# Attention's units laid between the slabs of the scan's r, k and v, in an encoder block on one core

## The reference, cut to what matters

```python
h_in = rms_norm(x, norm1_w)
z = h_in @ w_in                        # 4608 attention, 3360 scan, 4096 gate columns
z_attn, z_rwkv, z_gate = split(z)
# attention: 3 groups (dilation 1, 4, 16) of 8 heads of 64; q, k RMS-normed per head
for g, (window, dilation) in enumerate(((128, 1), (512, 4), (2048, 16))):
    o_g, lse_g = dilated_band_attention(q[:, :, g], k[:, :, g], v[:, :, g], dilation, 64, slopes[g])
o_attn = sum_g softmax_over_groups(lse)[g] * o_g
# scan: r, k, v and LoRA inputs are shifted over tokens; kk = k * k_k, unit length per head
zr = token_shift_centred(z_rwkv); ...
wkv = rwkv7_bidir_scan(r, decay, k_dir, v, kk, iclr)      # 16 heads, two directions
...
gates = sigmoid(z_gate + b_gate)       # 32 slabs of 128 columns
x = x + (gates[0] * (o_attn @ w_a) + gates[1] * (o_rwkv @ w_b)) @ w_out
x = x + swiglu(rms_norm(x, norm2_w))
```

## Time and profile before

| | |
|---|---|
| Device time, median of 3 runs | 3886.76 us (3876.7 to 3889.54) |
| The profiled execution | 3877.64 us |
| Its span, first to last instruction | 3875.9 us |
| Mean granted TensorE clock | 0.933 |
| PE busy | 3538.8 us, 91% |
| PE weight loads, DVE, ACT, POOL busy | 2882.6, 1642.1, 1056.4, 1637.7 us |
| DMA | 405.91 MB, mean 105 GB/s |

### The profile page before, as it was taken

The page is one execution under the profiler, slowest core; times in us unless marked ns, Lnnn a source line. Parts: engine busy times, 40 slices in busy tenths (PEclk is TensorE's granted clock), DMA queues, the critical chain, the costliest instruction groups (busy, mean ns, idle before and its releaser), DMA issues. The chain is left out here.

```text
span 3875.9 us, 45226 instructions
## 1 busy us (share of the span) xinstructions
PE 3538.8 (91%) x16478; PEld 2882.6 (74%) x16478; DVE 1642.1 (42%) x2026; ACT 1056.4 (27%) x1621; POOL 1637.7 (42%) x1347
## 2 busy tenths in 40 slices
PE   5999999886668899999857799999999999999999
PEld 4477788675545788888735577888888888888887
DVE  3066715663246777777523244332133123302321
ACT  4332211212332344444322212222222112212221
POOL 2133344231002877787713444344444444444433
PEclk8799999996558999999978999999999999999999
DMA  4433344331005555555243334233333333333333
GB/s 160 151 105 93 94 133 121 106 111 57 24 24 137 126 136 130 130 148 130 60 141 95 114 103 123 84 97 89 106 97 94 89 109 90 91 99 98 97 91 104
DMA packets 765541, 405.91 MB, mean 105 GB/s; under 512 B 191390, under 2 KB 726106, under 8 KB 764922
## 3 DMA queue, kind: packets, MB, share of 16 engines
q1 hardware_dynamic: 765434, 404.53, 36.1%
HBM read 345.73 MB, written 58.72 MB: 104 GB/s over the span
## 5 line engine op out<-in xcount | busy, mean ns | idle before, releaser
L131 POOL TENSOR_TENSOR w_lo_b<-w_raw_b,w_hi_b 128x2048 fp32r<-128x2048 f32 (+3 forms) x200 | 744.0, 3720 | 1014.0 <-ACT w_hi_b L124 1013.8
L140 PE MATMUL f_bank<-act_rounded,w_lo_b 128*128 128x512 f32 x1664 | 649.6, 390 | 21.6 <-POOL act_rounded L1896 13.8
L141 PE MATMUL f_bank<-act_rounded,w_hi_b 128*128 128x512 f32 x1664 | 648.8, 390 | 0.0
L142 PE MATMUL f_bank<-act_rounded,w_hi_b 128*128 128x512 f32 x1664 | 648.7, 390 | 0.0
L124 ACT CAST w_hi_b<-w_raw_b 128x2048 fp32r<-128x2048 f32 (+3 forms) x200 | 312.9, 1565 | 929.3 <-PE f_bank L142 858.6
L131 POOL TENSOR_TENSOR w_lo<-w_raw,w_hi 128x2048 fp32r<-128x2048 f32 x63 | 290.3, 4609 | 572.8 <-ACT w_hi L124 572.8
L140 PE MATMUL bank<-h_hi,w_lo 128*128 128x512 f32 x1008 | 404.8, 402 | 20.4 <-POOL w_lo L131 13.8
L142 PE MATMUL bank<-h_hi,w_hi 128*128 128x512 f32 x1008 | 395.7, 393 | 0.0
L141 PE MATMUL bank<-h_lo,w_hi 128*128 128x512 f32 x1008 | 395.5, 392 | 0.0
L140 PEld LDWEIGHTS f_bank<-act_rounded,w_lo_b 128*128 128x128 f32 x1664 | 313.3, 188 | 88.4 <-POOL act_rounded L1896 14.2
L142 PEld LDWEIGHTS f_bank<-act_rounded,w_hi_b 128*128 128x128 f32 x1664 | 313.2, 188 | 65.2
(11 more groups left out here) (319 smaller groups left out, 5444.2 us busy)
## 6 DMA issues: line engine op xcount, KB each, us to landing
w_raw<-in_w_in_dram SPq DMA_DIRECT2D x63, 1024.0 KB, 5.3
w_raw_b<-in_w_ffn_gate_dram SPq DMA_DIRECT2D x44, 1024.0 KB, 5.1
w_raw_b<-in_w_ffn_up_dram SPq DMA_DIRECT2D x44, 1024.0 KB, 5.2
w_raw_b<-in_w_ffn_down_dram SPq DMA_DIRECT2D x64, 704.0 KB, 4.5
gate_w_plain<-in_w_in_dram SPq DMA_DIRECT2D x64, 512.0 KB, 4.5
w_raw_b<-in_w_out_dram SPq DMA_DIRECT2D x16, 1024.0 KB, 5.7
zt<-out SPq DMA_DIRECT2D x60, 256.0 KB, 2.6
zt<-lout SPq DMA_DIRECT2D x40, 256.0 KB, 2.0
```

Of the source, the lines that this page charges most:

```text
L131: pool.tensor_tensor(g.w_lo[n.slot][:, 0:k, :], g.w_raw[n.slot][:, 0:k, :], g.w_hi[n.slot][:, 0:k, :].bitcast(F32), ALU.subtract).then_inc ...
L140: pe.matmul(bank, wl, hi[:, ka, :], start=start and j == 0, stop=False)
L141: pe.matmul(bank, wh, lo[:, ka, :], start=False, stop=False)
L142: ins = pe.matmul(bank, wh, hi[:, ka, :], start=False, stop=stop and j == len(ks) - 1)
```

## The change

The r, k and v slabs leave `phase_project` and go, with five slabs of the gates, into a new `phase_attention` of 29 slots with one slab each. Slots 0 to 11 also take scores, soft and exp of two units each, and the transpose, the weighted values and `file` of the two units before; slots 13, 15 and 16 (with 14 on DVE) the merge. Scores (`sc_ps`), `s_sb` and `p_t` have one buffer instead of two. Slabs come as p-th of r, p-th of k, p-th of v; a k slab's norm (`heads`, `floor`, `root`, `unit`) is done two slots later. Weights come in halves through a ring of five raw and four high halves. The order on each engine is written out per slot. Distances, slopes and masks are built at the end of `phase_setup` on POOL, after its two low parts. The scan keeps 27 gate slabs, so its last ten slots have none (before: five).

```diff
 def phase_setup(...):       # POOL
                 for c in range(2):
                     split_lo(pool, g, Step(c), KD)
+                attention_consts(pool, g, att_consts, dist_abs)
+                scan_masks(pool, g, made_masks)
...                          # DVE, after its last subtraction
+                dve.wait_ge(att_consts, 7)
+                for v in (g.dist[:, 0:3, :], g.dist[:, 3:5, 0:P]):
+                    dve.scalar_tensor_tensor(out=v, in0=v, scalar=-1.0, in1=v, op0=ALU.mult, op1=ALU.max).then_inc(dist_abs, 1)
...
-    NA, NB = 36, 24
-                (SB0, 8, "shift", COL_RKV, ROW_RKV, 24, None, 0),
-                (SB0 + 8, 8, "shift norm", COL_RKV + RW, ROW_RKV + RW, 24, "k_k", 8),
-                (SB0 + 16, 8, "shift", COL_RKV + 2 * RW, ROW_RKV + 2 * RW, 32, None, 16))
...
+N_SLAB = 3 * NPAIR
+EARLY_GATES = 5
+NGATE = 32 - EARLY_GATES
...
+N_SLOT = N_SLAB + EARLY_GATES
+RING = 5
+MERGE = N_ATT // 2 + 1
+
+def att_pe(s):
+    first = [("open", s, 4 if s == 0 else 0)]
+    if is_key(s - 2):
+        first.append(("heads", s - 2, 0))
+    for n in units_in(s):
+        first.append(("scores", n, 2))
+    for n in units_in(s - 1):
+        if n % ATT_PER_PAIR == 0:
+            j = n // ATT_PER_PAIR
+            first += [("turn_v0", j, 1), ("turn_v12", j, 1)]
+        first += [("turn_p", n, 4), ("sum", n, 0)]
+    if s == MERGE:
+        first += [("turn_rows", gr, 2) for gr in range(3)]
+    if s == MERGE + 2:
+        first += [("spread", n, 2) for n in range(8)]
+    if s == MERGE + 3:
+        first += [("spread", n, 2) for n in range(8, N_BC)]
+    return first
+
+def att_dve(s):
+    if 0 <= s - 1 < N_SLOT:
+        stages.append(("shift" if s - 1 < N_SLAB else "gate", s - 1))
+    if is_key(s - 2):
+        stages.append(("floor", s - 2))
+    for n in units_in(s):
+        stages.append(("soft", n))
+    for n in units_in(s - 1):
+        stages.append(("file", n))
+    if is_key(s - 2):
+        stages.append(("unit", s - 2))
...
+def att_act(s):
+    if is_key(s - 2):
+        stages.append(("root", s - 2))
+    for n in units_in(s):
+        if n % ATT_PER_PAIR == 0:
+            stages.append(("by_residue", n // ATT_PER_PAIR))
+    for i, n in enumerate(units_in(s - 1)):
+        if n % ATT_PER_PAIR == 0:
+            j = n // ATT_PER_PAIR
+            stages += [("take_v0", j), ("take_v12", j)]
+        stages.append(("take_p", n))
+        if i == 0:
+            stages.append(("high", 2 * s + 3))
+    if not units_in(s - 1):
+        stages.append(("high", 2 * s + 3))
+    for n in units_in(s):
+        stages.append(("exp", n))
+    if is_key(s - 1):
+        stages.append(("square", s - 1))
...
+    stages.append(("high", 2 * s + 4))
...                          # SP, per slot
+                    weights(2 * s + 4)
...                          # loads of the next pair's q, k, v
+                    weights(2 * s + 5)
+                    if 0 <= s - 1 < N_SLOT:
+                        sp.wait_ge(taken_dve, freed(x))
+                        sp.dma_start(zt[row:row + P, :], out[x % 2][:, :]).then_inc(out_stored[x % 2], 16)
+                    if is_key(s - 2):
+                        sp.wait_ge(taken_dve, ATT_DVE_AT["unit", s - 2])
...                          # DVE, soft
+                            dve.wait_ge(made, ATT_PE_AT["scores", n])
+                            if n >= 1:
+                                dve.wait_ge(taken_act, ATT_ACT_AT["exp", n - 1])
...                          # PE: scores, then sum
+                            if n >= 1:
+                                pe.wait_ge(taken_dve, ATT_DVE_AT["soft", n - 1])
...
+                            pe.wait_ge(taken_act, ATT_ACT_AT["take_p", n])
+                            if n >= 1:
+                                pe.wait_ge(taken_dve, ATT_DVE_AT["file", n - 1])
```

More of the change, by code:

```diff
@@ L590, in norm, with turn @@
                     link(dve.tensor_tensor(y[:, :], y[:, :], t_sb[:, :], ALU.mult))
[L591 to L604, removed]
+                    if not first:
+                        slot_free(st)
+                    dve.scalar_tensor_tensor(out=out[st.slot][:, :], in0=raw[st.slot][:, :], scalar=param(g, w),
+                                             in1=y[:, :], op0=ALU.mult, op1=ALU.mult).then_inc(g.out_ready, 1)
+                def turn(base, i, norms, w, first=False):
                     for j in range(UN):
@@ new lines, in att_dve @@
+def att_dve(s):
+    stages = []
+    if 0 <= s - 1 < N_SLOT:
[8 more added lines that the diff above has]
+        stages.append(("unit", s - 2))
+    if s == MERGE:
+        stages += [("rows", gr) for gr in range(3)] + [("less_top", gr) for gr in range(3)]
+    if s == MERGE + 1:
+        stages.append(("share", 0))
+    if s == MERGE + 2:
+        stages += [("weigh", n) for n in range(8)]
+    if s == MERGE + 3:
+        stages += [("weigh", n) for n in range(8, N_BC)]
+    return stages
@@ new lines, in att_act @@
+def att_act(s):
+    stages = []
+    if is_key(s - 2):
[16 more added lines that the diff above has]
+        stages.append(("square", s - 1))
+    if s == MERGE:
+        stages += [("exp_top", gr) for gr in range(3)]
+    stages.append(("high", 2 * s + 4))
+    return stages
@@ L1230, in phase_attention, with att_counts @@
+def att_counts(stages):
+    counts = {}
+    for s in range(N_SLOT + 1):
+        for st in stages(s):
+            if st[0] not in ("high", "open"):
+                counts[st[0], st[1]] = len(counts) + 1
+    return counts
+ATT_PE_AT, ATT_DVE_AT, ATT_ACT_AT = (att_counts(f) for f in (att_pe, att_dve, att_act))
+def phase_attention(nc, g, a, zt, oat):
+    w_in = a["w_in"].rearrange("l (k p) n -> (l p) k n", p=P)
     NP = ATTN_HPG // 2
+    H = ATTN_HPG
+    NH = 2 * N_SLOT
     with ExitStack() as ctx:
@@ new lines, in phase_attention, with two_banks @@
+        spare = [v for t in (s_sb, *p_sb, p_t) for v in halves(t)]
+        m_row, d_row, m_top, total = spare[0:3], spare[3:6], spare[6], spare[7]
+        def two_banks(t):
+            v = t[:, :, :].rearrange("p a b -> p (a b)")
+            return v[:, 0:SEQ], v[:, SEQ:2 * SEQ]
+        row_banks = (two_banks(sc_ps), two_banks(pt_ps), (pv_ps[:, :], heads_ps[:, :]))
+        spread_banks = two_banks(sc_ps) + two_banks(pt_ps)
+        made, taken_dve, taken_act, chain = sem("att_made"), sem("att_taken_dve"), sem("att_taken_act"), sem("att_chain")
@@ L1303, in _ @@
[L1303 to L1313 removed]
+                for h in range(NH):
+                    pool.wait_ge(hi_ready, h + 1)
+                    pool.tensor_tensor(raw_half(w_lo, h), raw_half(w_raw, h), hi_half(h).bitcast(F32), ALU.subtract).then_inc(lo_ready, 1)
```

781 lines of the change are left out of this document (425 added, 356 removed).

## The result

The changed kernel takes **3869.93 us** (median, 3855.48 to 3875.67, 14 runs), the kernel before 3894.69 us on the same chip (3874.58 to 3900.37, 14 runs): a ratio of **0.9938, 95% interval 0.9921 to 0.9955**. It gains 25 us where 78 were forecast, outside the range of 3750 to 3852. The profiled execution has a span of 3870.9 us; the kernel before had 3875.9.

The account below looks back on a forecast made before the run. PE bounds the slabs and gated scan; attention is a serial chain through PE, DVE and ACT, mostly at 1.2 GHz. Stretch -59.4, scan -27.6 and setup +8.6 sum to -78.4: 3808 us against the median, range 3750 to 3852.

Parts of the forecast that it names:

- The stretch: Last product of the last attention slab to the scan's first gate product: 604.2 us before, 544.8 forecast, -59.4.
- the forecast's signs of being right: Unit slots about 26, 32, 20 us; PE waiting for file and soft; bare slabs 10.88 apart; inversions without pause.
- Clock: Twelve unit slots of the new stage: about 1.3 us lost each, 16 us, taken from the old key slabs' stretch.
- Rival 3: PE stays at 1.2 GHz through the unit slots, +139 less the 16 already in: 3931; chance 0.06.
- PE work of the unit slots: Attention work in the new stage: 75.4 us for four pairs of heads, a 128-column record at 0.11.
- A product at 0.227: New stage's slabs: 512-column products 0.227 us apart, slabs 10.88 apart, 315.5 us for 29 slabs.
- The waits: Unit slots' loop through PE, DVE and ACT: 26.2, 31.7, 20.3; three slots 78.2 us with 52.4 of PE work.
- B: Unit slot with scores of group 1, sums of group 0, v turned: 31.7, PE waiting 8 us in one piece.
- Merge: New stage's slots 13 to 16: 13.6, 10.9, 21.1, 14.3, together 59.9 us; the fifth spread waits 2.
- Scan: Slots 21 to 30: POOL's inversions end at 45, 79.5, 114, 148.5; 157 us against 184.9 before, -27.6.
- the second (the scan gives less): Rival: the scan gives nothing back, ungated slots hanging on another limit; 3836 us; chance 0.13.
- the fourth: Rival: more waiting, DVE held up beside POOL, loads late, 4 us in each unit slot; 3856; chance 0.09.

Follow-up runs that it names:

- h1: g3 with four slab tiles instead of two behind a slot's first scores and two behind the second; ratio 0.9788 to the kernel before.
- g3: Changed kernel with DVE's file(n-2) moved between the two soft and a key's unit behind the first soft; ratio 0.9806 to the kernel before.
- f1: Changed kernel with unused bytes so projection and new-stage weight tiles start on multiples of 512 bytes; ratio 0.991 to the kernel before.
- e3: Kernel before with an unused 96-byte tile ahead of the weight tiles of setup and projection; 3905.11 us, ratio 1.0025.

## Why the prediction was wrong

Its sign, its bound and the shape of its mechanism were right; five terms were too small (clock, PE work, distance of products, merge, scan) and a sixth, the waits, too large. The step that failed most is the price of the clock. The stretch was to lose 59.4 and loses 24.6; that is 34.8 of the 57.7 us between the forecast 78.4 and the 20.7 of the table above. The scan has 9.6 more, setup 2.2, the attention slabs 2.1, the way to slot 21 1.1 and the last stretch 7.9, of which no term of the forecast spoke.

**Read right.** PE's first slab moved by 9.4 (forecast 8.6). The way into the new stage took 12.7 (13.1), the way out 10.5 (11.5). PE waited for `file` and `soft`, longest in the slots behind a key's `unit`. It never waited for a low part there. The early gates cost more than they returned. Of the forecast's signs of being right, bare slabs 10.88 apart and inversions without a pause did not come, and pauses between the last inversions were one of its signs of being wrong.

**Clock, "I take about 1.3 for each of the twelve unit slots, 16 us".** PE was at 1.2 GHz for 72.9 us of those slots, half of it lost: 36. The stretch of the old key slabs that I called nearest kept 0.91; I carried its loss over by the slab, where 0.91 over the 296.8 us of the walk would already have been 27, and the unit slots granted 0.88 and 0.89 over 332 us. Slot 0 is the worst of them, 26.0 us against 17.3, with 11.5 us at 1.2 GHz: the walk started it at full speed, though PE had stood idle on the way in. h1 shows that the placing matters beside the sum: in slots 3 to 11 the same 14 us of waiting goes with 34.1 us at 1.2 GHz in g3 and 13.7 in h1. Rival 3 was the right mechanism, at a fraction of its price.

**PE work of the unit slots, "0.11 a record for 128 columns".** Groups of the scores of groups 1 and 2 in slots 3 to 11 (line, engine, operation, tiles, shapes, count, then busy us, mean ns, idle before):

```profile
L1679 PE MATMUL sc_ps<-k_sb,q_sb 64*128 64x128 f32 x48 | 13.4, 434 | 13.4 <-DVE negmax L1591 13.4
L1679 PE MATMUL sc_ps<-k_r,q_r 64*128 64x128 f32 x48 | 6.8, 283 | 4.2 <-DVE negmax L1591 4.2
```

Group 1 reads q and k with a step of four elements, and its records start 0.236 us apart instead of 0.112: 64 records, 8 us over the stage. In the kernel before the groups looked alike:

```profile
L1341 PE MATMUL sc_ps<-k_sb,q_sb 64*128 64x128 f32 x64 | 17.9, 435 | 0.0
L1341 PE MATMUL sc_ps<-k_r,q_r 64*128 64x128 f32 x64 | 16.6, 438 | 0.0
```

But there group 2 ran at 1.2 GHz throughout, while some units of group 1 did not. One of each, their stretches (the granted clock is the third number from the end) and their rows:

```profile
945.60:947.60 2.00, 2.00 (x9) 1.95 (x8) 0.69 (x1) 0.00 (x0) 0.00 (x0) 1.00 0.00 0
951.00:952.90 1.90, 1.90 (x9) 1.78 (x8) 1.06 (x1) 0.48 (x4) 0.00 (x0) 0.50 0.00 0
```

```profile
945.65 2.24 PE L1341 MATMUL sc_ps<-k_sb,q_sb 64*128 64x128 f32 x8
...
951.05 2.07 PE L1341 MATMUL sc_ps<-k_r,q_r 64*128 64x128 f32 x8
```

The eight records of group 1 took 2.24 us at full speed, 0.236 apart, as they do in the new stage, so the forecast's own trace had this price. I took all records to gain by the clock. Turning v of group 1 has the step in its weights alone, and its records are 0.121 apart against 0.109 without a step; so the step in the weights explains little of the 0.236. The Trainium skill (Advanced Engine Details and Errata, "SBUF Cachelines") says that it takes at least two hits on a 16 byte line to hide the access; at this step each element has a line of its own, and the trace agrees with 0.236 against 0.112.

**A product at 0.227.** It was 0.234: +3.9 in the bare slabs, 2 in the attention slabs. The same 0.35 a slab would be some 6 in the other seventeen, but f1, with 0.227, took 253.7 in slots 3 to 11 against 254.2, so there little of it is seen. No row of the kernel before could show it; what could have was the list of tiles that the change puts ahead of the weights.

**The waits, "26.2, 31.7, 20.3".** They measured 27.6 to 29.6, 32.3 to 32.7 and 25.5 to 25.6 from slot 3 to 10, with 54 us of waits against my 72. The walk of the loop priced too much waiting and too little work, and the two hid each other in B, where the forecast fitted by luck.

**Merge, "13.6, 10.9, 21.1, 14.3".** They took 13.0, 20.2, 22.6 and 15.0, 10.9 more in all. I let only the fifth spread wait, and 2 us; it does not wait, but the first one waits 5.9 for `share` (it stands in the 20.2, as slots are counted). Around it PE was at 1.2 GHz for 6.8 us, and a record of spread took 0.53 us where 0.425 was priced.

Together the stage is 34.7 longer than forecast: unit slots 19.3 (11.7 of it in slots 0 to 2), slot 12 0.6, merge 10.9, bare slabs 3.9.

**Scan, "45, 79.5, 114 and 148.5".** POOL in the changed kernel, end of the first inversion behind slot 21 and start of the next:

```profile
1777.41 0.14 POOL L808 MEMSET blocks<- 32x32 f32 x1 [4.43 <-DMA blocks<-nb]
...
1813.70 0.23 POOL L817 TENSOR_TENSOR blocks<-blocks,inv_step 32x30 f32<-32x30 f32 x1
1819.76 0.15 POOL L808 MEMSET blocks<- 32x32 f32 x1 [5.83 <-DMA blocks<-nb]
```

The inversions last 36.5, 36.6, 36.0 and 34.3, and the second and fourth wait 5.8 and 2.3 for their blocks. I took the shortest, the old last one, for all but the first, and no pause, though the earlier trace rows had one of 5.68 in front of that very inversion. The first begins 10.4 after slot 21's start (forecast 9). Slots 21 to 30 take 168.3 and 165.4, where 157 were forecast. (184.9 less 157 is 27.9, not 27.6, and 904.79 to 913.26 is 8.5, not 8.6; neither matters here.) Spreading the ungated slots (one gate less in every two) was not tried.

**The base.** The profile was taken with its distance to the median named, but not its cause. The 15 us of the LoRA clock leave the forecast gain as it is, yet made the first comparison of traces point to a loss that was none.

Of the rivals the second (the scan gives less) was right in a third of its 27.6, the fourth in place (1.6 us more per unit slot, priced 4), the third in mechanism; none of them alone reaches the result.

## What to carry to other kernels

Where work is laid into gaps, PE pays for the waits that are left and, in these runs, in clock beside them: here a reordering of two DVE steps was worth twice the whole change. A price per record should be taken from records at the clock that the new place will have. When tiles are added ahead of weight tiles, look at where those then start; a few hundred unused bytes were worth an estimated 5 to 10 us. Before a sum is made from one profiled execution, see whether the stages' clocks are those of the median run.

## What the runs showed of the hardware

In uninterrupted slabs f32 products of 512 columns followed each other at 0.227 us where the weight tile starts on a multiple of 512 bytes and at 0.226 to 0.238 elsewhere; moving the tiles of the projection by 96 bytes, and nothing else, took it from 0.227 to 0.234 (e3). Records of 128 columns whose moving operand and weights are both read with a step of 16 bytes were 0.236 us apart at 1.2 and at 2.4 GHz alike, dense ones 0.214 and 0.112; with the step in the weights alone 0.121 against 0.109 at 2.4 GHz. The same program had PE at 1.2 GHz for 54.6 us in one execution and for 88.7 in two others, at the same place.
